# Stick-breaking attention by two sigmoids and a scan, and retention with its decay folded into q and k, in a one-core Trainium2 layer kernel

## The chip, the cores and the metric

The kernel runs on one NeuronCore of a Trainium2 chip. The metric is the device time of one launch in microseconds, median of several runs. The unchanged kernel took 957.01 us (three runs, 956.07 to 957.04).

## What is computed

One layer of a decoder with 512 tokens of 1024 features, in fp32: an RMSNorm, one wide projection, two token mixers of 8 heads each (stick-breaking attention with 64-wide heads, retention with 64-wide keys and 128-wide values), their gated merge, a convolutional GLU of width 2816, and a gated embedding. What the change touches are the two mixers:

```
# stick-breaking, strictly causal (s < t); q, k normed per head
z     = (q . k) / 8
A[t,s] = sigmoid(z[t,s]) * prod_{s<j<t} (1 - sigmoid(z[t,j]))
y     = A v
# retention, gamma_h = 1 - 2^(-5-h), q and k rotated
Y[n]  = sum_{m<=n} gamma_h^(n-m) (q_n . k_m) / 8  v_m
y_r   = rmsnorm_per_head(Y) * silu(g_r)
```

Tolerance asks for more than one fp32r pass: each operand is split into a rounded part `hi` and a rest `lo`, and each product is three matmuls (`split3`: hi.hi, hi.lo, lo.hi).

## The kernel before

Features lie on partitions, tokens along the free axis. The work is 128-column weight chunks: each chunk is eight k-steps of three matmuls of 512 columns into one of three `dense` banks. For each chunk ScalarE makes `w_hi`, VectorE `w_lo` (`ahead(j, s)` makes those of chunk s+2), SyncE loads `w_f` when the `w_lo` of two chunks earlier is done (`load`).

Heads are handled in four pairs j, with nine chunks (slots 0 to 8) a pair: stick-breaking q, k, v, retention q, k, two swish gates, two retention v. TensorE's order is written out by hand: small attention steps are hooks behind a given k-step of a given slot, written (slot, k) here. `back(j)` is slots 3 to 8 and carries the stick-breaking of pair j; `front(j)` is slots 0 to 2 and carries the retention of pair j-1. After the fourth pair, three gate chunks with the same hooks follow ("tail"). Pairs 1 to 3 are one loop, pair 0 is written apart. VectorE, ScalarE and SyncE have orders of their own, and each engine executes strictly in order, with semaphores between them.

Stick-breaking before (`sb_step`, lines 344 to 360): for one head and one block of 128 keys (8 units a pair, of 128 to 512 queries) TensorE makes z transposed (keys on partitions), and adds a mask with an extra matmul (L348). VectorE and ScalarE make softplus(z) (`sb_abs`, exp, ln, `sb_softplus`, a hi and a lo part). TensorE then adds minus the running sum over keys by matmuls with a triangular and an all-ones matrix (L358, 20 a head), ScalarE takes exp, and the weights, already transposed, go with v into `ybank` (`sb_values`). Three z banks keep three units in flight.

Retention before (`r_step`): for one head and one block of keys TensorE makes the scores, VectorE multiplies by a decay table (512 KB loaded a pair), hi and lo are made, and TensorE multiplies with v.

Rotation (`rotate`, `rotate_sum`) needs the two 32-row halves of each head exchanged. SyncE does that with four SBUF-to-SBUF DMAs (`swap_halves`, L208), which stand in its queue behind the weight load that waits for the `w_lo` of chunk 6 of the pair, which is VectorE's `ahead(j, 4)`.

Of the kernel before, what the change touches and what calls it, by code (L numbers as in the profile page):

```python
# [23 lines left out]
P = 128  # L24
# [31 lines left out]
T_SP, T_A = 27, 30  # L56
T_YQ = (28, 27)
# [8 lines left out]
A_RAW, A_SQ, A_SQY, A_SWAP, A_Y = 0, 2, (7, 3), 4, 5  # L66
A_DEC, A_COS, A_G, A_T, A_A = 8, 10, 12, 14, 16
A_SG = (10, 14, 8)
A_RS, A_ACC, A_CONV, A_C, A_SQR, A_U = 8, 9, 10, 12, 13, 16
A_RS2 = 6  # L70
A_P = 14
N_F32 = 18
H_ORDER = (0, 1, 2, 6, 4, 3, 5, 7)
# [9 lines left out]
def build(nc, xT, pT, w_in, w_a, w_b, w_out, w_up, w_down, w_pg, w_pp, g_mix, g_ffn, g_ple, g_ret, g_sbq, g_sbk,  # L83
          conv_w, conv_b, consts, decay, rope, outT):
    with ExitStack() as ctx:
# [3 lines left out]
        def sem(name):  # L89
# [10 lines left out]
        cr = sb("cr", [P, N_CONST, P], F32R)  # L100
# [23 lines left out]
        s_swap, s_rmul, s_rot, s_rhi = sem("s_swap"), sem("s_rmul"), sem("s_rot"), sem("s_rhi")  # L124
        s_misc = sem("s_misc")

        s_z, s_abs, s_e, s_l, s_sp, s_sphi, s_splo = (sem("s_z"), sem("s_abs"), sem("s_e"), sem("s_l"), sem("s_sp"),
                                                      sem("s_sphi"), sem("s_splo"))
        s_u, s_zx, s_ysum, s_yshi, s_yslo = sem("s_u"), sem("s_zx"), sem("s_ysum"), sem("s_yshi"), sem("s_yslo")
        s_ahi, s_alo = sem("s_ahi"), sem("s_alo")  # L130

        s_zr, s_zd, s_yr = sem("s_zr"), sem("s_zd"), sem("s_yr")
# [28 lines left out]
        def sb_unit(n):  # L161

            return n // NT, NT - 1 - n % NT

        def r_unit(n):

            return n // NT, n % NT

        def sp_cols(hd, i):

            at = 1280 if (hd == 1 and i == 3) else (0, 512, 896, 1152)[i]
            return at, at + width(i)

        def sp_view(t, hd, i):
            a, b = sp_cols(hd, i)
            return t[:, T_SP:T_SP + 3, :].rearrange("p t n -> p (t n)")[:, a:b]
# [5 lines left out]
        def _(sp):  # L182
# [14 lines left out]
            sp.dma_start(fs[:, A_COS:A_COS + 2, :], rope[:, :, :]).then_inc(s_rope, 16)  # L197
            for c in range(3, 8):
                load(c, c % RING, w_in[c], 8)
# [11 lines left out]
            def pair_loads(j, s):  # L211
                c = SLOTS * j + s + 5
                load(c, (s + 5) % RING, w_in[c], 8)
                if s == 4:
                    sp.wait_ge(s_h, 5)
                    swap_halves(j, 0)
                if s == 5:
                    swap_halves(j, 1)
                if s == 6:
                    sp.wait_ge(s_evac, SLOTS * j + 6)  # L220
                    sp.dma_start(fs[:, A_DEC:A_DEC + 2, :], decay[j]).then_inc(s_dec, 16)

# [62 lines left out]
        def _(pe):  # L285
# [21 lines left out]
            def stat(w, src, done):  # L307
                return mm(misc[:, :], cst[:, w, :], fs[:, src, :], start=True, stop=True).then_inc(done, 1)  # L308
# [7 lines left out]
            def stat_y(j, hd, free):  # L316

                pe.wait_ge(s_yqlo, 2 * j + hd + 1)
                pe.wait_ge(*free)
                mm(misc[:, :], cr[:, C_ONES, :], hi[:, T_YQ[hd], :], start=True, stop=False)  # L320
                mm(misc[:, :], cr[:, C_ONES, :], lo[:, T_YQ[hd], :], start=False, stop=True).then_inc(s_ystat, 1)

            def turn_v(j, s, free):
# [3 lines left out]
                for i in range(NT):  # L327
                    ins = nc.tensor.transpose(misc[:, i * P:(i + 1) * P],  # L328
                                              fs[:, A_RAW + RAW_OF[s] % 2, i * P:(i + 1) * P],
                                              cst[:, C_IDENT, :])  # L330
                ins.then_inc(s_vt, 1)

            def sb_step(j, n):

                if n < 8:
                    hd, i = sb_unit(n)
                    N = width(i)
                    if n == 0:
                        pe.wait_ge(s_raw_done, RAWS * j + 2)
                    if n >= 3:  # L340
                        pe.wait_ge(s_zx, 8 * j + n - 2)
                    rows = slice(64 * hd, 64 * hd + 64)
                    z = zbank[n % 3][:, 0:N]
                    keys, qs = slice(i * P, (i + 1) * P), slice(i * P, SEQ)
                    split3(z, hi[rows, T_SBK, keys], lo[rows, T_SBK, keys], hi[rows, T_SBQ, qs], lo[rows, T_SBQ, qs],
                           start=True, stop=False, skip=True)

                    mm(zbank[n % 3][:, 0:P], cr[:, C_IDENT, :], cr[:, C_MASK, :], start=False, stop=True,  # L348
                       skip_group_check=True).then_inc(s_z, 1)
                if n >= 2:  # L350
                    u = n - 2
                    hd, i = sb_unit(u)
                    N = width(i)
                    pe.wait_ge(s_splo, 8 * j + u + 1)
                    for ii in range(i, NT):
                        w = cr[:, C_NEGU if ii == i else C_NEG1, :]
                        for part in (hi, lo):
                            ins = mm(zbank[u % 3][:, (ii - i) * P:N], w, sp_view(part, hd, ii), start=False,  # L358
                                     stop=(ii == NT - 1 and part is lo), skip_group_check=True)
                    ins.then_inc(s_u, 1)  # L360

            def sb_values(j, v):

                _, i = sb_unit(v)
                if v == 0:
                    pe.wait_ge(s_raw_done, RAWS * j + 3)
                if v == 4:
                    pe.wait_ge(s_yslo, 2 * j + 1)
                pe.wait_ge(s_alo, 16 * j + v + 1)
                cols = slice(i * P, (i + 1) * P)  # L370
                ins = split3(ybank[:, i * P:SEQ], hi[:, T_SBV, cols], lo[:, T_SBV, cols],
                             hi[:, T_A + v % 2, 0:width(i)], lo[:, T_A + v % 2, 0:width(i)],
                             start=(v % NT == 0), stop=(v % NT == 3), skip=True)
                if v % NT == 3:
                    ins.then_inc(s_ysum, 1)

            def r_step(j, n):

                if n < 8:
                    hd, i = r_unit(n)  # L380
                    if n == 0:
                        pe.wait_ge(s_raw_done, RAWS * j + 5)
                    if n >= 3:
                        pe.wait_ge(s_zd, 8 * j + n - 2)
                    rows = slice(64 * hd, 64 * hd + 64)
                    keys, qs = slice(i * P, (i + 1) * P), slice(i * P, SEQ)
                    split3(zbank[n % 3][:, 0:width(i)], hi[rows, T_RK, keys], lo[rows, T_RK, keys], hi[rows, T_RQ, qs],
                           lo[rows, T_RQ, qs], start=True, stop=True).then_inc(s_zr, 1)
                if n >= 1:
                    v = n - 1  # L390
                    hd, i = r_unit(v)
                    if v == 0:
                        pe.wait_ge(s_yslo, 2 * j + 2)
                        pe.wait_ge(s_raw_done, RAWS * j + 6)
                    if v == 4:
                        pe.wait_ge(s_raw_done, RAWS * j + 7)
                        pe.wait_ge(s_yraw, 2 * j + 1)
                    pe.wait_ge(s_alo, 16 * j + 8 + v + 1)
                    cols = slice(i * P, (i + 1) * P)
                    ins = split3(ybank[:, i * P:SEQ], hi[:, T_RV + hd, cols], lo[:, T_RV + hd, cols],  # L400
                                 hi[:, T_A + v % 2, 0:width(i)], lo[:, T_A + v % 2, 0:width(i)],
                                 start=(i == 0), stop=(i == 3), skip=True)
                    if i == 3:
                        ins.then_inc(s_yr, 1)
# [4 lines left out]
            def front(j, prev):  # L409

                for s in range(3):
                    free_bank(j, s)
                    hooks = {1: lambda: r_step(prev, 3 * s), 4: lambda: r_step(prev, 3 * s + 1),
                             7: lambda: r_step(prev, 3 * s + 2)}
                    if s == 0:
                        hooks[6] = lambda: turn_v(prev, 8, (s_raw_done, RAWS * j - 1))
                    if s == 1:
                        hooks[5] = lambda: stat_qk(j, 0, (s_raw_done, RAWS * j))
                    if s == 2:
                        hooks[3] = lambda: stat_qk(j, 1, (s_misc, 4 * j - 1))  # L420
# [1167 lines left out]
```

## Time and profile before

| | us |
|---|---|
| median of three runs | 957.01 |
| span of the profiled execution | 955.7 |
| TensorE matmul busy | 941.7 |
| VectorE busy | 522.8 |
| ScalarE busy | 433.9 |

The span runs from the first to the last instruction of the profiled execution. The 1.3 us between it and the median lie around it. Matmuls are pipelined and overlap in the trace, so the duration of one says less than the distance from its start to the start of the next.

### The profile page before, as it was taken

How to read it: one execution, taken by the hardware profiler on the slowest of the kernel's cores; microseconds unless marked ns; L12 is line 12 of the kernel's file. 1: busy time of each engine (PE TensorE's matmuls, PEld its weight loads, DVE VectorE, ACT ScalarE, POOL GpSimd, SP SyncE). 2: the span in 40 equal slices, each digit the busy share in tenths (PEclk: the TensorE clock that was granted, in tenths of full speed). 3: DMA queues.
4: the chain of work that ended last, by engine and by line, in shares of the span. 5: the costliest groups of instructions: out<-in, count | busy, mean ns of one | idle time of the engine just before them, and what ended most of it. 6: DMA issues, size and time to landing. Idle time of an engine off the chain costs nothing.

```text
span 955.7 us, 12085 instructions
## 1 busy us (share of the span) xinstructions
PE 941.7 (99%) x4214; PEld 756.9 (79%) x4214; DVE 522.8 (55%) x741; ACT 433.9 (45%) x662; POOL 4.0 (0%) x11
## 2 busy tenths in 40 slices
PE   6999999999999999999999999999999999999998
PEld 4777778778777878888878788888888888888786
DVE  6887575566566544333355565655656553333354
ACT  6566676477566644222334533333333332222422
POOL 1000000000000000000000000000000000000000
PEclk9999999999999999999999999999999999999999
DMA  7232122122213114332232233232232333332232
GB/s 258 70 110 67 57 77 88 44 77 89 75 44 110 50 50 177 117 103 78 86 124 97 90 109 110 88 107 90 88 108 89 98 89 99 88 96 87 76 122 82
DMA packets 27851, 89.95 MB, mean 94 GB/s; under 512 B 3728, under 2 KB 4768, under 8 KB 27696
## 3 DMA queue, kind: packets, MB, share of 16 engines
q1 hardware_dynamic: 27168, 86.91, 27.9%
q10 hardware_dynamic: 432, 2.63, 0.8%
q8 instruction: 16, 0.26, 0.1%
q0 software_dynamic: 224, 0.06, 0.0%
q14 instruction: 11, 0.09, 0.0%
HBM read 85.39 MB, written 2.10 MB: 92 GB/s over the span
## 4 chain that ended last, share of the span: by engine, by line
PE 96%; DVE 2%; ACT 1%; DMA 1%; issue 0%; SPq 0%; DVEq 0%; ACTq 0%
PE dense L290 28%; PE dense L292 27%; PE dense L291 27%; PE z L290 2%; PE z L358 2%; PE ybank L290 2%; PE z L292 1%; PE ybank L291 1%; PE z L291 1%; PE ybank L292 1%; PE z L348 1%; PE misc L308 1%; DVE fs L1009 1%; DMA fs<-in_xT 1%; PE misc L328 1%; DVE w_lo L1009 1%
## 5 line engine op out<-in xcount | busy, mean ns | idle before, releaser
L290 PE MATMUL dense<-hi,w_hi 128*128 128x512 f32 x1184 | 472.0, 399 | 9.8 <-DVE lo L1012 9.4
L291 PE MATMUL dense<-lo,w_hi 128*128 128x512 f32 x1184 | 462.6, 391 | 0.0
L292 PE MATMUL dense<-hi,w_lo 128*128 128x512 f32 x1184 | 462.4, 391 | 0.0
L1009 DVE TENSOR_TENSOR w_lo<-w_f,w_hi 128x1024 fp32r<-128x1024 f32 (+2 forms) x160 | 184.5, 1153 | 241.8 <-ACT w_hi L581 241.5
L290 PEld LDWEIGHTS dense<-hi,w_hi 128*128 128x128 f32 x1184 | 223.2, 189 | 57.7 <-issue 12.8
L292 PEld LDWEIGHTS dense<-hi,w_lo 128*128 128x128 f32 x1184 | 222.9, 188 | 47.2
L291 PEld LDWEIGHTS dense<-lo,w_hi 128*128 128x128 f32 x1184 | 223.3, 189 | 45.3 <-issue 2.6
L581 ACT CAST w_hi<-w_f 128x1024 fp32r<-128x1024 f32 (+2 forms) x160 | 158.3, 990 | 184.2 <-PE dense L292 182.1
L566 ACT ACTIVATE fs<-fs 128x512 f32<-128x512 f32 (+5 forms) x151 | 87.1, 580 | 99.6 <-DVE fs L1009 41.8
L1009 DVE TENSOR_TENSOR lo<-fs,hi 128x512 fp32r<-128x512 f32 (+4 forms) x167 | 94.5, 576 | 56.7 <-ACT hi L944 20.1
L1009 DVE TENSOR_TENSOR fs<-fs 128x512 f32<-128x512 f32 x99 | 67.4, 687 | 2.5 <-DMA fs<-fs 0.3
L1009 DVE TENSOR_TENSOR fs<-dense,fs 128x512 f32<-128x512 f32 x84 | 57.5, 684 | 8.7 <-ACT fs L566 5.0
L1012 DVE SCALAR_TENSOR_TENSOR fs<-fs,cw 128x512 f32<-128x512 f32 x44 | 33.1, 752 | 28.0 <-ACT fs L566 25.0
L944 ACT CAST hi<-fs 128x512 f32 (+1 forms) x22 | 13.7, 621 | 59.5 <-DVE fs L1009 59.5
L566 ACT ACTIVATE fs<-fs,cw 128x512 f32<-128x512 f32 x22 | 17.9, 816 | 43.8 <-DVE fs L1009 43.8
L1009 DVE TENSOR_TENSOR fs<-z,fs 128x512 f32<-128x512 f32 (+3 forms) x32 | 15.7, 489 | 31.2 <-PE z L292 31.2
L647 ACT CAST hi<-fs 128x512 fp32r<-128x512 f32 (+3 forms) x32 | 14.7, 460 | 38.4 <-DVE fs L1009 38.4
L1012 DVE SCALAR_TENSOR_TENSOR lo<-fs,gain,hi 128x512 fp32r<-128x512 f32 (+1 forms) x24 | 17.7, 750 | 25.1 <-ACT hi L566 25.1
L290 PEld LDWEIGHTS z<-hi 64*128 64x128 f32 x64 | 11.7, 183 | 23.0 <-issue 22.1
L290 PE MATMUL z<-hi 64*128 64x128 f32 (+3 forms) x64 | 26.2, 410 | 0.2 <-DVE lo L1009 0.2
L1012 DVE SCALAR_TENSOR_TENSOR fs<-z,fs 128x128 f32<-128x128 f32 (+3 forms) x32 | 15.7, 489 | 16.0 <-ACT fs L566 15.8
L290 PE MATMUL ybank<-hi 128*128 128x128 f32 (+3 forms) x64 | 22.6, 353 | 0.0
(67 smaller groups left out, 497.9 us busy)
## 6 DMA issues: line engine op xcount, KB each, us to landing
w_f<-in_w_in SPq DMA_DIRECT2D x52, 512.0 KB, 3.3
w_f<-in_w_up SPq DMA_DIRECT2D x44, 512.0 KB, 3.2
w_f<-in_w_down SPq DMA_DIRECT2D x16, 512.0 KB, 3.5
w_f<-in_w_b SPq DMA_DIRECT2D x8, 512.0 KB, 3.3
w_f<-in_w_out SPq DMA_DIRECT2D x8, 512.0 KB, 3.3
w_f<-in_w_pg SPq DMA_DIRECT2D x8, 512.0 KB, 3.3
w_f<-in_w_down SPq DMA_DIRECT2D x8, 384.0 KB, 3.0
fs<-in_xT SPq DMA_DIRECT2D x4, 512.0 KB, 7.6
```

The lines of the kernel that those rows point to most:

```text
L290: mm(out, w1, x1, start=start, stop=False, skip_group_check=skip)
L291: mm(out, w1, x0, start=False, stop=False, skip_group_check=skip)
L292: return mm(out, w0, x1, start=False, stop=stop, skip_group_check=skip)
L308: return mm(misc[:, :], cst[:, w, :], fs[:, src, :], start=True, stop=True).then_inc(done, 1)
L328: ins = nc.tensor.transpose(misc[:, i * P:(i + 1) * P], fs[:, A_RAW + RAW_OF[s] % 2, i * P:(i + 1) * P], cst[:, C_IDENT, :])
L358: ins = mm(zbank[u % 3][:, (ii - i) * P:N], w, sp_view(part, hd, ii), start=False, stop=(ii == NT - 1 and part is lo), skip_group_check=True)
L566: return nc.scalar.activation(out, src, func, **kw).then_inc(done, 1)
L581: nc.scalar.copy(w_hi[r][:, 0:kt, :], w_f[r][:, 0:kt, :]).then_inc(s_whi, 1)
L647: nc.scalar.copy(hi[:, T_A + n % 2, 0:width(i)], fs[:, A_A + n % 2, 0:width(i)]).then_inc(s_ahi, 1)
L944: nc.scalar.copy(hi[:, T_G + f, :], fs[:, A_U, :]).then_inc(s_ghi, 1)
L1009: return nc.vector.tensor_tensor(out, a, b, op).then_inc(done, 1)
L1012: return nc.vector.scalar_tensor_tensor(out=out, in0=a, scalar=scalar, in1=b, op0=op0, op1=op1).then_inc(done, 1)
```

## The change

Stick-breaking now works on a block of 128 queries (i = 3, 2, 1, 0), with queries on partitions and all its keys (512, 384, 256, 128) along the free axis, for both heads of the pair at once. The scores of the two heads alternate matmul by matmul, one on array rows 0 to 63, the other on 64 to 127, into two banks `z`. ScalarE takes sigmoid(z) into SBUF and sigmoid(-z) in place in PSUM. VectorE scans the latter over the keys from the last to the first (one `tensor_tensor_scan` a head, 511 to 127 elements) and multiplies. TensorE transposes the weights back with the identity (20 transposes of 128 x 128 a pair), ScalarE and VectorE make hi and lo, and the value matmuls are those of before. The mask matmul, the triangular sums, and the softplus go.

Retention: q is multiplied by gamma^t and k by its inverse (`decayed`), so that the scores need only a 128 x 128 causal mask on the diagonal block. Both heads go together here too. The decay table shrinks to two rows of factors (`load_fac`). The steps behind retention (`y_raw`, `y_square`, `norm_y`, `y_swish`, `low_y`) take both heads in one instruction. A preload of the sigmoid tables is added a pair. There is one z buffer where there were three.

The core of the diff:

```diff
+            def heads_scores(i, w, x, cols, at):
+                for (wp, xp), first, last in (((hi, hi), True, False), ((hi, lo), False, False),
+                                              ((lo, hi), False, True)):
+                    for hd in range(2):
+                        rows = slice(64 * hd, 64 * hd + 64)
+                        ins = mm(z[:, hd, 0:cols.stop - cols.start], wp[rows, w, i * P:(i + 1) * P], xp[rows, x, cols],
+                                 start=first, stop=last)
+                ins.then_inc(at, 1)
...
+            def sb_scores(j, i):
...
+                    pe.wait_ge(s_scan, 8 * j + 2 * (NT - 1 - i))
...
+            def sb_turn(j, i):
...
+                    pe.wait_ge(s_atlo, NT * j + (NT - 1 - i))
+                pe.wait_ge(s_a, NT * j + NT - i)
...
+                places = {(5, 2): at(sb_scores, j, 2), (5, 4): at(sb_turn, j, 3), (5, 7): at(sb_scores, j, 1),
+                          (6, 1): at(sb_turn, j, 2), (6, 2): at(sb_values, j, 0, 3), (6, 3): at(sb_scores, j, 0),
+                          (6, 5): at(sb_turn, j, 1), (6, 6): at(sb_values, j, 0, 2), (7, 0): at(sb_turn, j, 0),
+                          (7, 2): at(sb_values, j, 0, 1), (7, 4): at(sb_values, j, 0, 0), (7, 7): at(sb_values, j, 1, 3),
+                          (8, 0): at(sb_values, j, 1, 2), (8, 1): at(sb_values, j, 1, 1), (8, 2): at(sb_values, j, 1, 0),
+                          (8, 6): at(turn_v, j, 7, (s_atlo, NT * j + NT))}
...
+                    places[3, 3] = at(turn_v, j, 2, (s_misc, 3 * j + 1))
+                    places[3, 4] = at(sb_scores, j, 3)
+                    places[3, 7] = at(stat_y, prev, (s_raw_done, RAWS * j + 3))
...
+            def sb_factors(j, i):
+
+                n = NT - 1 - i
+                act.wait_ge(s_z, NT * j + n + 1)
+                if n or not isinstance(j, int):
+                    act.wait_ge(s_tr, NT * j + n)
+                zz = z[:, :, 0:keys(i)]
+                run(fs[:, A_AT:A_AT + 2, 0:keys(i)], zz, ACT.Sigmoid, s_beta)
+                act.wait_ge(s_beta, NT * j + n + 1)
+                run(zz, zz, ACT.Sigmoid, s_f, scale=-1.0)
...
             def back(j, prev):
                 evac(j, 2)
                 ahead(j, 3)
-                sb_early(j, 0)
                 high_v(j, 0)
...
+                norm_y(prev, 3 * j + 2)
+                sigmoid_tables()
+                evac(j, 3)
+                sb_factors(j, 3)
+                high_y(prev)
                 ahead(j, 4)
...
                 evac(j, 4)
+                sb_factors(j, 2)
+                sb_high(j, 3)
                 ahead(j, 5)
...
+            def sb_weights(j, i):
...
+                for hd in range(2):
+                    nc.vector.tensor_tensor_scan(fs[:, A_CP + hd, 1:N], z[:, hd, N - 1:0:-1], mrev[:, 0:N - 1], 0.0,
+                                                 ALU.mult, ALU.max).then_inc(s_scan, 1)
+                dve.wait_ge(s_scan, 8 * j + 2 * n + 2)
+                a = fs[:, A_AT:A_AT + 2, 0:N]
+                tt(a, a, fs[:, A_CP:A_CP + 2, N - 1::-1], ALU.mult, s_a)
...
+            def turned(j, t):
+                rotate(j, t)
+                rotate_sum(j, t)
+                decayed(j, t)
...
             def back(j, prev):
                 ahead(j, 3)
...
                 low_v(j, 0)
+                y_norm(prev)
+                y_swish(prev)
+                sb_weights(j, 3)
+                low_y(prev)
+                ahead(j, 4)
+                turned(j, 0)
+                sb_weights(j, 2)
+                sb_low(j, 3)
+                ahead(j, 5)
+                low_rot(j, 0)
+                sb_weights(j, 1)
+                sb_low(j, 2)
+                sb_weights(j, 0)
+                ahead(j, 6)
+                sb_low(j, 1)
+                turned(j, 1)
                 sb_low(j, 0)
...
```

## Rows read from the trace of the kernel before

**Rows 1.** The page: engine totals, granted clock by slices, chain that ended last.

```profile
PE 941.7 (99%) x4214; PEld 756.9 (79%) x4214; DVE 522.8 (55%) x741; ACT 433.9 (45%) x662; POOL 4.0 (0%) x11
...
PEclk9999999999999999999999999999999999999999
...
PE 96%; DVE 2%; ACT 1%; DMA 1%; issue 0%; SPq 0%; DVEq 0%; ACTq 0%
```

**Rows 2.** TensorE's waits: waiter, whom it waited for, total us, times, longest.

```profile
PE dense L290 <- DVE lo L1012: 9.4, 3, 8.7
```

**Rows 3.** TensorE timeline (start, us, instruction): last matmuls before borders of phases.

```profile
81.94 0.40 PE L292 MATMUL ybank<-hi,lo 128*128 128x512 f32 x1
...
111.83 0.27 PE L292 MATMUL ybank<-hi,lo 128*128 128x128 f32 x1
...
193.10 0.27 PE L292 MATMUL ybank<-hi,lo 128*128 128x128 f32 x1
...
353.94 0.27 PE L292 MATMUL ybank<-hi,lo 128*128 128x128 f32 x1
```

**Rows 4.** TensorE timeline around a score step, a transpose group, mask and triangular sums.

```profile
83.31 0.39 PE L292 MATMUL dense<-hi,w_lo 128*128 128x512 f32 x1
...
84.85 0.40 PE L291 MATMUL dense<-lo,w_hi 128*128 128x512 f32 x1
...
116.20 0.60 PE L328 MATMUL misc<-cst,fs 128*128 128x128 f32 x4
116.55 0.48 PE L290 MATMUL dense<-hi,w_hi 128*128 128x512 f32 x1
116.87 0.39 PE L291 MATMUL dense<-lo,w_hi 128*128 128x512 f32 x1
...
136.83 0.33 PE L348 MATMUL z<-cr 128*128 128x128 f32 x1
137.00 0.45 PE L358 MATMUL z<-hi,cr 128*128 128x512 f32 x1
...
137.52 0.34 PE L358 MATMUL z<-hi,cr 128*128 128x384 f32 x1
...
137.87 0.28 PE L358 MATMUL z<-hi,cr 128*128 128x256 f32 x1
...
138.11 0.23 PE L358 MATMUL z<-hi,cr 128*128 128x128 f32 x1
...
138.28 0.45 PE L290 MATMUL dense<-hi,w_hi 128*128 128x512 f32 x1
```

**Rows 5.** Instruction groups by shape, first 360 us: busy us, mean ns | idle.

```profile
L566 ACT ACTIVATE fs<-fs 128x512 f32<-128x512 f32 x49 | 30.5, 629 | 5.2 <-DVE fs L1152 4.2
L566 ACT ACTIVATE fs<-fs 128x1024 f32<-128x1024 f32 x4 | 4.2, 1059 | 0.0
L570 ACT ACT_TABLE_LOAD x5 | 6.4, 1283 | 1.3 <-DVE eps L1020 1.2
...
L1009 DVE TENSOR_TENSOR w_lo<-w_f,w_hi 128x1024 fp32r<-128x1024 f32 x41 | 50.2, 1224 | 24.1 <-ACT w_hi L581 23.9
L1009 DVE TENSOR_TENSOR lo<-fs,hi 128x512 fp32r<-128x512 f32 x57 | 38.9, 688 | 23.6 <-ACT hi L689 12.5 <-ACT hi L647 6.4 <-ACT hi L630 2.1
```

**Rows 6.** Timelines of VectorE and SyncE, pair 0: w_lo, exchange DMAs, first use.

```profile
46.65 1.23 DVE L1009 TENSOR_TENSOR w_lo<-w_f,w_hi 128x1024 fp32r<-128x1024 f32 x1 [0.26 <-ACT w_hi L581]
...
48.51 2.50 SPq L208 DMA_DIRECT2D fs<-fs  x4
...
52.67 1.29 DVE L1009 TENSOR_TENSOR fs<-fs 128x512 f32<-128x512 f32 x2 [0.29 <-DMA fs<-fs]
```

**Rows 7.** TensorE timeline at the start: the first matmul, and where spacing changes.

```profile
8.68 0.77 PE L290 MATMUL dense<-hi,w_hi 128*128 128x512 f32 x1 [8.68 <-DVE lo L1012]
...
14.79 0.40 PE L292 MATMUL dense<-hi,w_lo 128*128 128x512 f32 x1
15.03 0.40 PE L290 MATMUL dense<-hi,w_hi 128*128 128x512 f32 x1
```

More of the change, by code:

```diff
@@ L55 @@
 T_RQ, T_RK, T_RV = 23, 24, 25
-T_SP, T_A = 27, 30
-T_YQ = (28, 27)
+T_AT = 27
+T_YQ = 27
 T_X0 = 8
@@ L159, in a_sq, with keys, flat, at_blocks @@
             return A_T + t if isinstance(j, int) else A_SQ
[L161 to L176, printed above, removed]
+        def keys(i):
+            return P * (i + 1)
+        def flat(t):
+            return t[:, T_AT:T_AT + 5, :].rearrange("p t n -> p (t n)")
+        def at_blocks(t):
+            return flat(t).rearrange("p (h b c) -> p h b c", h=2, b=10)
+        def at_row(t, hd, kb):
+            first = 10 * hd + (0, 4, 8, 7)[kb]
+            return flat(t)[:, first * P:first * P + width(kb)]
+        def r_pair(t, i):
+            at = T_AT + 2 * (i % 2)
+            return t[:, at:at + 2, 0:width(i)]
+        def yq(t):
+            return t[:, T_YQ:T_YQ + 2, :]
+        def norm_y_pair():
+            return fs[:, A_SQY:A_SQY + 5:4, :]
         block = ctx.enter_context(nc.Block())
@@ L331, in turn_v @@
                 ins.then_inc(s_vt, 1)
[L333 to L360, printed above, removed]
@@ L374, in sb_values @@
[L374 to L404, printed above, removed]
@@ new lines, in sb_values, with r_scores @@
+                pe.wait_ge(s_atlo, NT * j + NT - kb)
+                cols = slice(kb * P, (kb + 1) * P)
+                ins = split3(aty[:, 2, kb * P:SEQ], hi[:, T_SBV, cols], lo[:, T_SBV, cols], at_row(hi, hd, kb),
+                             at_row(lo, hd, kb), start=(kb == NT - 1), stop=(kb == 0), skip=True)
+                if kb == 0:
+                    ins.then_inc(s_ysum, 1)
+            def r_scores(j, i):
+                if i == 0:
+                    pe.wait_ge(s_raw_done, RAWS * j + 5)
+                    pe.wait_ge(s_scan, 8 * j + 8)
+                else:
+                    pe.wait_ge(s_ralo, NT * j + i)
+                heads_scores(i, T_RK, T_RQ, slice(i * P, SEQ), s_zr)
@@ new lines, in r_values @@
+            def r_values(j, i):
+                if i == 0:
+                    pe.wait_ge(s_yslo, 2 * j + 2)
+                    pe.wait_ge(s_atlo, NT * j + NT)
+                    pe.wait_ge(s_raw_done, RAWS * j + 7)
+                pe.wait_ge(s_ralo, NT * j + i + 1)
+                cols = slice(i * P, (i + 1) * P)
+                for hd in range(2):
+                    ins = split3(aty[:, 1 + hd, i * P:SEQ], hi[:, T_RV + hd, cols], lo[:, T_RV + hd, cols],
+                                 r_pair(hi, i)[:, hd, :], r_pair(lo, i)[:, hd, :], start=(i == 0), stop=(i == NT - 1),
+                                 skip=True)
+                ins.then_inc(s_vr, 1)
@@ L411, in front @@
                 for s in range(3):
                     free_bank(j, s)
[L413 to L420, printed above, removed]
-                        hooks[6] = lambda: stat_y(prev, 0, (s_misc, 4 * j))
@@ L422, in front @@
[L422 to L436 removed]
+                    chunk(first_chunk + s, s, s, KD, T_H, {k: places[s, k] for k in range(KD) if (s, k) in places})
@@ L462, in _ @@
             with pe.Fori(1, PAIRS) as j:
-                front(j, j - 1)
+                front(j, j - 1, SLOTS * j)
                 back(j, j - 1)
             last = PAIRS - 1
-            for s in range(3):
-                free_bank(PAIRS, s)
-                hooks = {1: lambda: r_step(last, 3 * s), 4: lambda: r_step(last, 3 * s + 1),
-                         7: lambda: r_step(last, 3 * s + 2)}
-                if s == 0:
-                    hooks[5] = lambda: turn_v(last, 8, (s_raw_done, RAWS * PAIRS - 1))
-                if s == 2:
-                    hooks[3] = lambda: stat_y(last, 0, (s_raw_done, RAWS * PAIRS))
-                chunk(GATE0 + s, s, s, KD, T_H, hooks)
+            front(PAIRS, last, GATE0, tail=True)
             pe.wait_ge(s_gate, 1)
-            chunk(GATE0 + 3, 0, 0, KD, T_H, {3: lambda: stat_y(last, 1, (s_misc, 4 * PAIRS - 1))})
+            chunk(GATE0 + 3, 0, 0, KD, T_H, {5: lambda: stat_y(last, (s_raw_done, RAWS * PAIRS))})
             def branch_a(c, r, m):
@@ L738, in front @@
-                y_square(prev, 0)
-                evac(j, 1)
-                r_high(prev, 6)
                 high_qk(j, 0)
-                norm_qk(j, 1, 4 * j)
-                r_high(prev, 7)
+                ahead(j, 2)
+                norm_qk(j, 1, 3 * j + 1)
+                y_raw(prev)
                 high_qk(j, 1)
-                ahead(j, 2)
-                norm_y(prev, 0, 4 * j + 1)
-                y_raw(prev, 1)
-                y_square(prev, 1)
+                y_square(prev)
@@ new lines, in y_norm, with y_swish @@
+            def y_norm(j):
+                dve.wait_ge(s_yrs, j + 1)
+                for hd in range(2):
+                    y = fs[:, A_Y + hd, :]
+                    col = G_RET + hd + 2 * j
+                    stt(y, y, gain[:, col, :], norm_y_pair()[:, hd, :], ALU.mult, ALU.mult, s_yn)
+            def y_swish(j):
+                y = fs[:, A_Y:A_Y + 2, :]
+                dve.wait_ge(s_silu, j + 1)
+                dve.wait_ge(s_yn, 2 * j + 2)
+                tt(y, y, fs[:, A_G:A_G + 2, :], ALU.mult, s_yf)
@@ new lines, in low_y @@
+            def low_y(j):
+                dve.wait_ge(s_yrhi, j + 1)
+                pair = bass.ds(T_YR + 2 * j, 2)
+                tt(lo[:, pair, :], fs[:, A_Y:A_Y + 2, :], hi[:, pair, :], ALU.subtract, s_yrlo)
+            def sb_weights(j, i):
+                n = NT - 1 - i
+                N = keys(i)
+                dve.wait_ge(s_f, NT * j + n + 1)
+                if n or not isinstance(j, int):
+                    dve.wait_ge(s_a, NT * j + n)
+                for hd in range(2):
+                    nc.vector.tensor_tensor_scan(fs[:, A_CP + hd, 1:N], z[:, hd, N - 1:0:-1], mrev[:, 0:N - 1], 0.0,
[3 more added lines that the diff above has]
+                tt(a, a, fs[:, A_CP:A_CP + 2, N - 1::-1], ALU.mult, s_a)
@@ L1303, in back @@
-                ahead(j, 5)
-                sb_step(j, 5)
-                low_rot(j, 0)
-                ahead(j, 6)
-                sb_step(j, 6, lambda: y_low(j, 0))
-                sb_step(j, 7, lambda: rotate(j, 1), lambda: rotate_sum(j, 1))
+                y_norm(prev)
[7 more added lines that the diff above has]
+                ahead(j, 5)
```

560 lines of the change are left out of this document (243 added, 317 removed).

## The prediction

> **What bounds the kernel now.** First the page: TensorE is busy 99% of the span and makes 96% of the chain that ended last [rows 1]. Busy time of pipelined matmuls can hide waits, so next the list of TensorE's waits: one large one, 8.7 us before the first matmul, and almost nothing after it [rows 2]. The hand-written order covers every wait, so time is the sum of matmul spacings, and a microsecond taken from TensorE's work would be one gained if the cover held. Third, the phase borders [rows 3]. Slot 3 of pair 1 starts behind 111.83, that of pair 2 behind 193.10: a pair takes 81.3 us. Slot 0 of pair 1 starts at 82.2 (81.94 and one spacing), so a front takes 29.8 and a back 51.5. The attention is over at 354, behind 353.94; what follows isn't changed. A dense matmul of 512 columns is spaced 0.227 us, a k-step is 0.68, a slot 5.46.
>
> **What TensorE loses and gains** [rows 4]. Mask: 136.83 to 137.00, 0.17 each, 8 a pair: 1.4. Triangular sums, a hi and a lo matmul each: 0.52 for 512 columns (137.00 to 137.52), 0.35 for 384, 0.24 for 256, 0.17 for 128. A head needs 1, 2, 3 and 4 of these: 2.62; two heads 5.2. Score step: from 83.31 to 84.85 lie 1.54 us with two dense spacings in them, so a 512-column step costs 1.09: three matmuls of 0.227, and 0.41 for going to 64-row matmuls and back. With 0.17, 0.12 and 0.11 for the shorter ones, four steps of a head cost 3.5 and a mixer's two heads 7.0.
>
> After the change a mixer has four entries instead of eight. No row shows two matmuls on different array halves. If head 1 costs nothing beside head 0, a mixer costs 3.5; if they queue up, 3.5 + 1.9 = 5.4. I take 3.5: operands lie on separate row halves, results in separate banks, and nothing in a 64-row matmul uses the other half. The Trainium skill (TensorE: Matmul & The Clock Gate, Part 3) has such matmuls start nearly together; no run here shows it yet.
>
> Added transposes: 116.20 to 116.55 is 0.0875 each, the next dense one comes 0.09 late; 20 in four groups: 2.1. Values, statistics and v transposes keep their matmuls. Saved a pair: 1.4 + 5.2 + 2 x 3.5 - 2.1 = 11.5, of it 3.5 in the front; four pairs 46 us. A pair would be 69.8.
>
> **Whether the cover holds.** ScalarE costs about 0.20 + 0.84 ns an element, a table load 1.28, VectorE 0.15 + 1.05 ns an element [rows 5]. In total both get less: stick-breaking takes two sigmoids and a cast where it took five passes, and one scan, one product and one subtraction where it took four. But the work is now one chain with one z buffer: the scores of block i wait for both scans of block i+1, the sigmoids wait for that block's transposes. Three units in flight hid this before.
>
> The scan has no row. Below is one tensor_tensor: 0.69 for 512. Above I take two cycles an element, since each result needs a multiply and then a max of the one before it: 0.15 + 2 x 1.05 ns, so 1.23, 0.96, 0.69, 0.42 us for 512 to 128. I use the upper end. The Trainium skill (DVE: opcode table, instruction layouts, handler registers and perf-mode slots, Datapath and trigger behaviour) says the built-in scan runs at half throughput. Its figure would be this same 1.23; no row bears on it.
>
> A steady back, zero at the end of slot 3, where `stat_y` has just run. ScalarE, strictly in order: `norm_y` (two of 1024) to 2.4, sigmoid tables 3.7, `evac` 4.2, two sigmoids of 1024 to 6.4. VectorE: two scans to 8.8, product 10.0, `low_y` 11.2, `ahead(j, 4)` 12.4. That last one releases the SyncE load with the four exchange DMAs behind it, and VectorE's next instruction, `rotate`, wants them landed. From the end of that `w_lo` (46.65 + 1.23 = 47.9) to the first rotation, which waited for the DMA at 52.67, are 4.8 us [rows 6]. Before, this lay under other work; now VectorE stands to 17.2. Rotation and decay (four of 0.69) last to 20.2, and only then come the scans of block 2, to 22.1. Behind the waiting instruction are queued these scans, `sb_low(j, 3)` and `ahead(j, 5)`.
>
> TensorE meanwhile: slot 4 to 5.5, three k-steps to 7.5, waits 1.3 for the first scans, scores 0.9, two k-steps, transposes 0.8, three k-steps: 13.9. Its scores of block 1 at (5, 7) wait for the scans at 22.1: **8.2 us**. Further on: at (6, 3) two sigmoids of 512 and two scans of 256 take 2.85 behind the transposes, covered by 1.7: 1.15. At (7, 0) 3.9 (sigmoids, scans, product, `ahead`, `sb_low(j, 1)`) are covered by 2.4: 1.5. At (7, 7) the values of head 1 wait for `y_low`, behind a silu with table loads on both sides: 1.6. At (3, 3) `turn_v` waits for an `evac` behind `y_square`: 0.4. Sum 14.2 a pair, against 11.5 saved.
>
> Pair 0 has another order, with scans of block 2 ahead of the rotation. There I walk to 1.8 at (5, 7), 5.2 at (6, 3) (the rotation, `ahead` and `evac_x` stand before its scans), 0.5 at (7, 0) and 3.5 at (7, 7): 11. The tail keeps its cover: `stat_y` to `low_y` is some 7.3 us, against 8.2 us of matmuls.
>
> **The clock.** After its 8.7 us of standing idle TensorE ran 14 spacings in 6.1 us, 0.43 each, which is 512 columns at 1.2 GHz, and then 0.24 and 0.23, at 2.4 GHz [rows 7]. The page's granted clock doesn't show it, its first slice is as full as all others [rows 1]. That start lost 14 x 0.2 = 2.9 us. A wait of 8.2 us resembles it; some of the loss is taken up by the waits just behind, so I count 2.0 a pair and 1.0 in pair 0: 7 us. The bounds are 0 and 4 x 2.9 = 12. The Trainium skill (TensorE: Matmul & The Clock Gate, Part 1) says that an idle array goes back to half clock. That rule speaks against this change: without it the sum below ends 7 us lower.
>
> **The sum** against the profiled 955.7: -46 + 3 x 14.2 + 11 + 7 = +14.6, a span of 970.3. The median lies 1.3 above the span: 971.6, say 971.5. The smaller decay load (DMA queues are mostly idle) and the added constants at the start, where VectorE has 8 us of matmuls ahead of it, I put at nothing; without that cover the latter would be 2 us.
>
> **The rivals.**
> - *The long wait is short; faster.* One mechanism: VectorE comes to the scans of block 2 earlier. If the scan streams like a tensor_tensor, each pair's waits fall by 2.6 (10 us in all), and then, with the exchange landed within 3.2 us instead of 4.8, by 1.6 more in three pairs (5); TensorE stands less than 6 us at a time and the clock stays up (7). 971.5 - 22 = 949.5. It decides where a pair's waits sum to less than 11.5, that is, where the wait at (5, 7) is under 5.5 us. For it: every wait here is from a walk of four queues, and back-to-back instructions overlap by 0.1. Against it: the exchange is tied to `ahead(j, 4)` and VectorE stands right behind it. Chance 0.22.
> - *The two heads queue up.* 1.9 a mixer more, in the fronts on TensorE, in the backs on the chain: 15 more, 986.5. For it: no row shows overlap. Chance 0.13.
> - *TensorE's work alone counts*, as it does before: 957 - 46 = 911. Against it is the single z buffer. Chance 0.04.
> - *Losses meet gains*, within 0.2%: 957. Chance 0.05.
> - The forecast, 971.5 with its own range from 960 (fast scan) to 980: chance 0.56.
>
> **How the numbers follow.** Faster is 0.22 + 0.04 = 0.26, same 0.05, slower 0.56 + 0.13 = 0.69. About 0.2% is what a measurement of this kernel can tell from no change. The range runs from 946, which takes in the faster rival and leaves out the lone TensorE case, to 988, which takes in the queueing heads.
>
> **What would show it.** Right: TensorE's largest waits are z <- DVE scan, about 8 us three times, with VectorE idle for 4 to 5 us on DMA fs<-fs just before; a pair of about 86 us; scans of 1.2 us for 512; matmuls spaced 0.43 behind the long waits; the two heads' score matmuls starting nearly together. Wrong: a wait at (5, 7) under 5.5 us, scans of 0.7, or spacing of 0.227 straight after the wait. A pair below 81 us makes the sign wrong.

## The result, and the profile after

The changed kernel takes 971.3 us (median of 4 runs, 968.87 to 973.42) against 956.96 (4 runs) for the kernel before on the same chip. The ratio is 1.0152, with a 95% interval of 1.0135 to 1.017: slower by 14.4 us, where 971.5 was forecast. The profiled execution spans 969.4 us against 955.7. This is its page (engine totals, granted clock by slices, chain that ended last); it answers to [rows 1]:

```profile
PE 908.7 (94%) x4102; PEld 733.5 (76%) x4102; DVE 511.8 (53%) x653; ACT 395.8 (41%) x517; POOL 4.0 (0%) x11
...
PEclk9999989998999999999999999999999999999999
...
PE 81%; ACT 7%; DVE 6%; issue 3%; DMA 1%; SPq 1%; ACTq 0%; DVEq 0%
```

TensorE, VectorE and ScalarE all have less to do than before, and yet the span grew. TensorE went from 99% busy to 94%, and its share of the chain from 96% to 81%; what it lost went to ScalarE, VectorE, the issue of instructions and the exchange DMA. Two slices of the clock row show an 8. All of it lies in the first 370 us, the attention.

TensorE's waits (waiter, whom it waited for, total us, times, longest). Before there was one group that mattered [rows 2]:

```profile
PE z L366 <- DVE fs L1155: 33.9, 11, 7.4
...
PE dense L314 <- DVE lo L998: 9.0, 3, 8.3
PE aty L314 <- DVE lo L995: 7.6, 4, 3.1
PE aty L393 <- DVE lo L995: 5.2, 4, 1.5
```

`PE dense L314` is the old wait ahead of the first matmul. The other three are new, 46.7 us together: scores waiting for the scan, values and transposes waiting for a low half.

The phase borders of [rows 3] are now here (TensorE timeline: start, us, instruction):

```profile
112.21 0.27 PE L316 MATMUL aty<-hi,lo 128*128 128x128 f32 x1
...
197.39 0.27 PE L316 MATMUL aty<-hi,lo 128*128 128x128 f32 x1
```

A pair takes 85.2 us (197.39 - 112.21, and 85.3 for the next one, which ends at 282.69) instead of 81.3: 3.9 more. The last matmul of the attention starts at 366.05 where it did at 353.94, 12.1 later. The border isn't at the same place in the order, though: from it to the first matmul of the same later stage (496.16 before, 509.85 after), the windows hold 626 and 634 matmuls. Columns: window, us, PE busy (count), PEld, DVE, ACT, POOL, clock, DMA share, GB/s; first before, then after.

```profile
353.94:496.16 142.22, 141.82 (x626) 116.83 (x626) 57.81 (x69) 47.92 (x62) 0.00 (x0) 1.00 0.34 113
```

```profile
366.05:509.85 143.80, 143.40 (x634) 118.41 (x633) 58.49 (x67) 49.97 (x61) 0.00 (x0) 1.00 0.32 112
```

Both are full but for 0.4 us, and the second is 1.6 longer, by eight more matmuls: the same work, cut at another place. So 12.1 + 1.6 = 13.7 is what the attention costs more, and it is all of the difference of the spans. Three pairs of 3.9 and 2.0 in pair 0 make it up.

Now one back, that of pair 1, on TensorE. The last bracket is the idle time before the row, and who ended it:

```profile
130.73 0.44 PE L366 MATMUL z<-hi 64*128 64x384 f32 x2 [1.06 <-DVE fs L1155]
...
143.34 0.58 PE L366 MATMUL z<-hi 64*128 64x256 f32 x2 [7.27 <-DVE fs L1155]
...
144.28 0.79 PE L314 MATMUL dense<-hi,w_hi 128*128 128x512 f32 x1
144.87 0.63 PE L315 MATMUL dense<-lo,w_hi 128*128 128x512 f32 x1
145.29 0.63 PE L316 MATMUL dense<-hi,w_lo 128*128 128x512 f32 x1
...
147.84 0.39 PE L315 MATMUL dense<-lo,w_hi 128*128 128x512 f32 x1
148.06 0.39 PE L316 MATMUL dense<-hi,w_lo 128*128 128x512 f32 x1
...
150.43 0.33 PE L366 MATMUL z<-hi 64*128 64x128 f32 x2 [0.94 <-DVE fs L1155]
...
156.96 0.43 PE L393 MATMUL aty<-cst,fs 128*128 128x128 f32 x2 [1.52 <-DVE lo L995]
...
164.97 0.33 PE L314 MATMUL aty<-hi 128*128 128x128 f32 x1 [1.52 <-DVE lo L995]
```

Five waits, 12.3 us. Behind the long one the dense matmuls start 0.42 apart (144.87, 145.29; the next two 0.43 each) and by 147.84 are 0.22 apart again. Here the granted clock shows it, which it didn't at the start [rows 7] (windows, columns as above; 0.52 here, 1.00 again from 147 to 150):

```profile
143.30:147.00 3.70, 3.66 (x13) 2.81 (x14) 3.68 (x5) 0.00 (x0) 0.00 (x0) 0.52 0.01 2
```

And VectorE with SyncE's queue over the same stretch; it answers to [rows 6]:

```profile
128.34 2.33 DVE L1155 TENSOR_TENSOR_SCAN fs<-z,mrev 128x511 f32<-128x511 f32 x2 [1.06 <-ACT z L586]
...
131.85 1.22 DVE L995 TENSOR_TENSOR lo<-fs,hi 128x1024 f32 x1
132.99 1.22 DVE L995 TENSOR_TENSOR w_lo<-w_f,w_hi 128x1024 fp32r<-128x1024 f32 x1
138.83 2.02 DVE L995 TENSOR_TENSOR fs<-fs 128x512 f32<-128x512 f32 x3 [4.62 <-DMA fs<-fs]
...
141.49 1.79 DVE L1155 TENSOR_TENSOR_SCAN fs<-z,mrev 128x383 f32<-128x383 f32 x2
```

```profile
134.38 0.33 SPq L203 DMA_DIRECT2D w_f<-in_w_in  x1
134.84 2.46 SPq L232 DMA_DIRECT2D fs<-fs  x4
```

VectorE ends its `w_lo` at 134.2. Only then does SyncE issue the weight load and, behind it, the four exchange DMAs. VectorE's next instruction wants them and stands 4.6 us; rotation and decay follow, then the scans of block 2 to 143.3, and at 143.34 TensorE gets its scores. Two scans of 511 take 2.33.

### The profile page after: what moved, and what is told of

Its sections match the earlier page's. It is cut to its first block, busy times and chain, and to the rows that moved or that the text cites. A ratio compares the mean times of both kernels' runs of the same rounds, so it can differ in the third digit from the quotient of the medians.

```text
span 969.4 us, 11519 instructions
## 1 busy us (share of the span) xinstructions
PE 908.7 (94%) x4102; PEld 733.5 (76%) x4102; DVE 511.8 (53%) x653; ACT 395.8 (41%) x517; POOL 4.0 (0%) x11
## 4 chain that ended last, share of the span: by engine, by line
PE 81%; ACT 7%; DVE 6%; issue 3%; DMA 1%; SPq 1%; ACTq 0%; DVEq 0%
PE dense L314 25%; PE dense L316 24%; PE dense L315 24%; ACT fs L586 2%; PE z L366 2%; DVE fs L1155 2%; DVE fs L995 1%; DVE w_lo L995 1%; DVE lo L995 1%; ACT w_hi L601 1%; PE aty L314 1%; PE aty L332 1%; PE aty L316 1%; PE aty L315 1%; ACT z L586 1%
## 5 line engine op out<-in xcount | busy, mean ns | idle before, releaser
L314 PE MATMUL dense<-hi,w_hi 128*128 128x512 f32 x1184 | 476.6, 402 | 9.4 <-DVE lo L998 9.0
L314 PEld LDWEIGHTS dense<-hi,w_hi 128*128 128x128 f32 x1184 | 224.2, 189 | 62.7 <-issue 16.5
L995 DVE TENSOR_TENSOR fs<-fs 128x512 f32<-128x512 f32 (+3 forms) x115 | 82.9, 726 | 18.9 <-DMA fs<-fs 13.7
L586 ACT ACTIVATE fs<-fs 128x512 f32<-128x512 f32 (+2 forms) x79 | 55.4, 707 | 81.1 <-DVE fs L995 42.0
L995 DVE TENSOR_TENSOR lo<-fs,hi 128x512 fp32r<-128x512 f32 (+3 forms) x63 | 48.1, 765 | 41.5 <-ACT hi L930 20.1
L366 PE MATMUL z<-hi 64*128 64x512 f32 (+3 forms) x64 | 13.9, 432 | 34.0 <-DVE fs L1155 33.9
L366 PEld LDWEIGHTS z<-hi 64*128 64x128 f32 x64 | 6.3, 194 | 46.4 <-DVE fs L1155 38.6
L930 ACT CAST hi<-fs 128x512 f32 (+1 forms) x22 | 13.7, 621 | 59.5 <-DVE fs L995 59.5
L1155 DVE TENSOR_TENSOR_SCAN fs<-z,mrev 128x511 f32<-128x511 f32 (+3 forms) x32 | 24.5, 807 | 18.9 <-ACT z L586 18.8
L998 DVE SCALAR_TENSOR_TENSOR fs<-fs,gain 128x512 f32<-128x512 f32 x24 | 17.5, 748 | 29.6 <-ACT fs L586 29.6
L586 ACT ACTIVATE fs<-z 128x1024 f32<-128x1024 f32 (+3 forms) x16 | 11.3, 706 | 45.8 <-PE aty L393 45.8
L670 ACT CAST hi<-z 128x1024 fp32r<-128x1024 f32 (+3 forms) x16 | 11.1, 694 | 40.9 <-DVE z L995 40.9
```

Source lines behind the costliest of these rows:

```text
L314: mm(out, w1, x1, start=start, stop=False, skip_group_check=skip)
L366: ins = mm(z[:, hd, 0:cols.stop - cols.start], wp[rows, w, i * P:(i + 1) * P], xp[rows, x, cols], start=first, stop=last)
L586: return nc.scalar.activation(out, src, func, **kw).then_inc(done, 1)
L670: nc.scalar.copy(r_pair(hi, i), z[:, :, 0:width(i)]).then_inc(s_rahi, 1)
L930: nc.scalar.copy(hi[:, T_G + f, :], fs[:, A_U, :]).then_inc(s_ghi, 1)
L995: return nc.vector.tensor_tensor(out, a, b, op).then_inc(done, 1)
```

## Experiments

The theory: the loss is one chain in each back (exchange, rotation, scans, scores), whose cost is a wait of some 7 us and the clock behind it; TensorE's work really is smaller, and the two heads overlap. The rivals: the heads don't overlap; they do so only as neighbours in the program; the rotation itself, not the exchange, is what is late; the clock costs nothing; the waits belong to the new form and can't be covered.

### The exchange ahead of the weight load

```
             c = SLOTS * j + s + 5          # on SyncE
-            load(c, (s + 5) % RING, w_in[c], 8)
             if s == 4:
                 sp.wait_ge(s_h, 4)
                 swap_halves(j, 0)
+            load(c, (s + 5) % RING, w_in[c], 8)
             if s == 5:
                 swap_halves(j, 1)
```

Only in slot 4 does the order change: the exchange of `q` goes ahead of the load, that of `k` in slot 5 stays behind it. The exchange reads the retention `q` as ScalarE copied it out of the `dense` bank, and that is there well before the ring's buffer is free.

> Edit: SyncE issues the four exchange DMAs of pair j's q ahead of the weight load that waits for chunk 6's w_lo, no longer behind it. Theory (VectorE stands for the exchange in front of the scans of block 2): VectorE's 4.6 us of waiting for DMA fs<-fs vanish, TensorE's wait at (5, 7) falls from 7.3 to about 2.6 us in pairs 1 to 3, matmuls behind it stay at 0.227 apart, so 4.7 + 1 us a pair: about 955 instead of 971. Rival (one z buffer and one weight buffer make the chain of scores, sigmoids, scans and transposes too long by itself; the exchange only fills time that would be waited anyway): the wait at (5, 7) stays above 5.5 us, time 967 or more.

956.2 us, ratio 0.9997 (0.9987 to 1.0007): level with the kernel before, 15.1 less than the changed one. SyncE now issues the exchange at 127.31, where it was 134.84, and the first rotation follows its predecessor at once (SyncE, then VectorE):

```profile
127.31 2.46 SPq L232 DMA_DIRECT2D fs<-fs  x4
```

```profile
133.93 1.22 DVE L995 TENSOR_TENSOR w_lo<-w_f,w_hi 128x1024 fp32r<-128x1024 f32 x1
135.07 2.02 DVE L995 TENSOR_TENSOR fs<-fs 128x512 f32<-128x512 f32 x3
```

The long wait fell from 7.3 to 2.6 in all three pairs (the third is 2.59 at 298.76). Of the others only two are shorter, the 0.95 behind it in pair 2 (0.40) and the 0.65 in pair 0 (not in the list any more). TensorE timeline:

```profile
139.58 0.39 PE L366 MATMUL z<-hi 64*128 64x256 f32 x2 [2.56 <-DVE fs L1155]
...
218.78 0.39 PE L366 MATMUL z<-hi 64*128 64x256 f32 x2 [2.59 <-DVE fs L1155]
```

Three times 4.7 is 14 of the 15 us. So the order of two entries in SyncE's queue decides between slower and level. Not all of the clock came back, which the windows behind the three waits show (columns as above): in pair 1 it stays up, in pairs 2 and 3 it doesn't. From border to border the three pairs are 5.9, 5.3 and 4.7 us shorter (79.3, 80.0 and 78.7), so beyond the waits it was pair 1 that got something back, 1.2, and the others at most 0.2. Pair 0 ended 0.9 later, as more matmuls behind its waits ran slowly.

```profile
139.50:146.00 6.50, 5.44 (x34) 4.01 (x35) 5.82 (x10) 2.00 (x4) 0.00 (x0) 1.00 0.28 88
218.70:226.00 7.30, 6.82 (x34) 5.33 (x35) 5.83 (x10) 2.01 (x4) 0.00 (x0) 0.77 0.31 104
298.70:306.00 7.30, 6.30 (x31) 4.82 (x31) 5.37 (x9) 1.99 (x4) 0.00 (x0) 0.77 0.34 100
```

### The rotation behind the next unit

```
-                turned(j, 0)
                 ...            # scans of block 2 and sb_low(j, 3)
+                turned(j, 0)
```

> Edit: VectorE's rotation and decay of q in pairs 1 to 3 move behind the scans and the lo parts of block 2, as in pair 0; nothing else. Theory: the wait at (5, 7) falls to about 1.5 to 2 us, but ScalarE's rounding of the rotated q stands ahead of block 1's sigmoids, so the wait at (6, 3) grows from 0.9 to about 4.3; sum 3.5 less a pair and no slow matmuls, 957 to 960. Rival (chain too long by itself): the wait at (5, 7) stays above 5.5, 968 or more.

961.9 us, ratio 1.0063 (1.0047 to 1.008), a little above the 957 to 960 expected. VectorE does the scans while the exchange is under way. The long wait is 1.6, and one of 3.5 stands at the next scores:

```profile
136.19 0.39 PE L366 MATMUL z<-hi 64*128 64x256 f32 x2 [1.57 <-DVE fs L1155]
...
144.59 0.33 PE L366 MATMUL z<-hi 64*128 64x128 f32 x2 [3.53 <-DVE fs L1155]
```

The expectation had no slow matmuls either; behind the 3.53 the granted clock was 0.69 (144.5 to 150). The reason for the wait is on ScalarE, which works strictly in order: its `high_rot`, the cast of the rotated block, stands ahead of the next sigmoids, and now waits for the later rotation.

```profile
141.02 0.62 ACT L654 CAST hi<-fs 128x512 fp32r<-128x512 f32 x1 [4.78 <-DVE fs L995]
...
142.02 0.60 ACT L586 ACTIVATE fs<-z 128x512 f32<-128x512 f32 x1
```

Two cures of the same wait, by different means, bring 15 and 9 us. Both leave the rotation's four instructions as long as they were, and the first also leaves them where they were, ahead of the scans: so it is the exchange that was late. What one engine gains by a step moved back, the engine that takes its result next has to pay for, if its own order stays.

### Filling the wait

Ahead of the wait at (5, 7) TensorE gets 28 matmuls whose results nobody reads, in pairs 1 to 3. They change nothing that is waited for.

```
+                    if i == 1 and not isinstance(j, int):
+                        pe.wait_ge(s_yraw, j)
+                        for _ in range(28):
+                            mm(aty[:, 2, :], ones_r[:, :], hi[:, T_H, :], start=True, stop=True)
```

> Edit: in pairs 1 to 3, 28 matmuls of 512 columns with no use (6.4 us at 0.227) are put in front of the wait at (5, 7), into a bank that is overwritten afterwards; the output is unchanged. Theory (idling drops the clock): the scores behind the wait and the six dense matmuls after them stay at 0.227 instead of 0.43, about 1.5 us a pair less: 966 to 968. Rival (the slow spacing is no matter of idling, or the lost time is covered by the next wait): 971, within 1.5.

966.8 us, ratio 1.0115 (1.0098 to 1.0132): 4.6 less than the changed kernel, by adding work. In the profiled spans it is 964.0 against 969.4, 5.4 less. What is left of the wait is 0.98, and the dense matmuls behind it start 0.23 apart behind the first one (TensorE timeline):

```profile
142.15 0.39 PE L366 MATMUL z<-hi 64*128 64x256 f32 x2 [0.98 <-DVE fs L1159]
...
143.04 0.39 PE L315 MATMUL dense<-lo,w_hi 128*128 128x512 f32 x1
143.27 0.39 PE L316 MATMUL dense<-hi,w_lo 128*128 128x512 f32 x1
```

From border to border the three pairs take 84.0, 83.9 and 81.9 us instead of 85.2, 85.3 and 83.4, which puts the price of the clock alone at 1.2 to 1.5 us a pair. The other 1.2 of the 5.4 lie in pair 0, where the program is the same in both kernels: there behind the wait of 3.06 the clock stayed up in this execution and fell in the other. The experiment also confirms that the end of the wait is set elsewhere, since TensorE could do 28 more matmuls in it.

### The heads in turn, and the heads apart

First, all three matmuls of head 0 and then those of head 1 (before: the two heads alternate):

```
-                for (wp, xp), first, last in ...:
-                    for hd in range(2):
+                for hd in range(2):
+                    for (wp, xp), first, last in ...:
```

> Edit: the six score matmuls of a block run head 0's three first, then head 1's three, where they alternated. Theory (heads overlap only if neighbours in the order lie on different array halves): a mixer costs 1.9 us more on TensorE, 7.5 in the four fronts and a like amount on the chain in the backs: 979 to 986. Rival (TensorE overlaps what it finds in its queue, in whatever order, or the overlap is worth nothing): 971, within 2.

971.8 us, ratio 1.0161 (1.0144 to 1.0178), as the changed kernel. The rows are a surprise: in this program head 1's first matmul stands behind all of head 0's, and still the two first ones form one group, ahead of the second ones.

```profile
87.20 0.39 PE L316 MATMUL dense<-hi,w_lo 128*128 128x512 f32 x1
87.52 0.51 PE L366 MATMUL z<-hi 64*128 64x512 f32 x2
87.85 0.41 PE L366 MATMUL z<-lo,hi 64*128 64x512 f32 x2
88.08 0.41 PE L366 MATMUL z<-hi,lo 64*128 64x512 f32 x2
88.42 0.51 PE L314 MATMUL dense<-hi,w_hi 128*128 128x512 f32 x1
88.76 0.40 PE L315 MATMUL dense<-lo,w_hi 128*128 128x512 f32 x1
```

From the dense matmul ahead to the second one behind are 1.56 us (88.76 - 87.20), 1.55 in the changed kernel, and 1.54 with one head in the kernel before [rows 4]. So the heads ran side by side in either order, and the theory's half sentence that they have to be neighbours fell. The edit thus couldn't price the overlap, and a second one had to keep them apart: head 1 comes one dense k-step after head 0.

```
+                one_head(0)
+                late.append(lambda: one_head(1).then_inc(at, 1))   # run behind the next k-step
```

> Edit: in every block of scores, stick-breaking's and retention's, head 1's three matmuls come one dense k-step after head 0's, so that a full-array matmul stands between the halves; all else as in the changed kernel. Theory (the halves share time, in whatever order they stand, as long as nothing of the full array lies between them; a mixer of 3.5 us becomes the 7.0 of the kernel before): 14 us more in the four fronts, and in the backs 0.7 to 1.7 us more in front of each of four links of the chain, 12 to 18 us over four pairs: 995 to 1005. Rival (the overlap is worth little, the entries were the price): 975 to 983.

999.3 us, ratio 1.0456 (1.0439 to 1.0474), within the 995 to 1005 expected. Each head is now a step of its own:

```profile
91.80 0.49 PE L370 MATMUL z<-hi 64*128 64x512 f32 x1
...
93.59 0.50 PE L370 MATMUL z<-hi 64*128 64x512 f32 x1
```

The span grew by 27.5 us although the waits of the scores shrank by 6.0 (27.9 instead of 33.9). That is 33.5 us for 32 more steps, 1.05 each, where the forecast's 3.5 for four steps of all sizes gives 0.88. Of the rest, some 5 us, half is the clock: behind the long waits 7 or 8 dense spacings are slow where 5 were, 2.0 to 2.2 us above 0.227 in sum and not 1.2, which is 2.6 in three pairs and leaves about 1.0 a step. The other half isn't traced. Side by side, the second head costs nothing that can be seen.

### All orders

Is 11.5 us a pair of TensorE's work saved, and are the waits a matter of order alone? The last kernel computes the same with the same instructions, in another order: the exchange ahead of the load as above, and each unit of the back given more cover.

```
 back, TensorE:  scores of block 1 (5, 7) -> (6, 1), of block 0 (6, 3) -> (6, 7)
                 transposes (6, 1) -> (6, 3), (6, 5) -> (7, 2), (7, 0) -> (7, 5)
                 values of head 1 (7, 7)..(8, 2) -> (8, 4)..(8, 7); stat_y (3, 7) -> (3, 5)
 VectorE:        turned(j, 0) behind sb_low(j, 1), turned(j, 1) behind y_low(j, 0),
                 ahead(j, 6) ahead of sb_weights(j, 0), low_v ahead of ahead(j, 3)
 ScalarE:        high_rot(j, 0) behind sb_high(j, 0), y_high(j, 0) and the evac ahead of silu,
                 high_rot(j, 1) behind silu, high_v ahead of ahead(j, 3)
```

This is the edit in short; the values of head 0 move to match, and pair 0 has the same pattern.

> Edit: orders alone. The exchange DMAs ahead of the weight load; VectorE's rotations and ScalarE's rounding of rotated q and k behind the chain of scans; `stat_y` at (3, 5); the hooks of blocks 2 to 0 spread over slots 5 to 8, so that every link of the chain has 2 to 4 k-steps of cover; silu and its table loads behind the rounding of head 0's output. Theory (TensorE's saved work is real and only the waits ate it): a pair of 70 to 73 us instead of 85, waits under 3 us a pair, 918 to 932 us, faster than both kernels. Rival (the chain is too long for its six slots whatever the order): waits of 6 us or more a pair remain, 945 or more.

918.7 us, ratio 0.9609 (0.9593 to 0.9625): 37.5 us faster than the kernel before on the same chip (956.2), 52.6 faster than the changed one, by order alone. TensorE's waits are

```profile
PE dense L314 <- DVE lo L1002: 9.1, 3, 8.4
PE aty L393 <- DVE lo L999: 1.5, 4, 0.4
...
PE z L366 <- DVE fs L1159: 1.0, 5, 0.2
```

and a whole pair, at full clock throughout:

```profile
124.35:196.04 71.69, 70.92 (x353) 55.04 (x354) 46.97 (x62) 42.67 (x60) 0.00 (x0) 1.00 0.25 77
```

A pair is 71.7, with 0.6 of waits in it, so TensorE's work in a pair is 71.1 and the saving 81.3 - 71.1 = 10.2.

## Why the prediction was right

The number came out within 0.2 us. Its terms did not, though the mechanism did: one chain of exchange, rotation, scans and scores, whose waits eat more than TensorE saves. This is how they stand (us, in the profiled execution, with the sign of what they add):

```
                                       forecast   measured
TensorE's work, 4 pairs                 -46.0      -40.8   (-10.2 each)
waits, pairs 1 to 3                     +42.6      +36.8   (12.3 each)
waits, pair 0                           +11.0       +9.9
clock                                    +7.0       +7.8   (the rest; 1.8 each and 2.3)
span                                    +14.6      +13.7
```

The rest of pair 0 also holds the start, where the wait ahead of the first matmul was 0.4 shorter (8.29 and not 8.68).

*The saving: 11.5 forecast, 10.2 measured.* This step was mis-sized. Going to 64-row matmuls and back was priced at 0.41 for all 16 head steps of a pair, but in 8 of them the matmul behind the step was the mask. Its 0.17 [rows 4] was priced whole, and held part of the way back: among the values 128 columns take 0.06 to 0.11. So 0.05 to 0.1 for each of the 8 was counted twice. The transposes cost 1.95 and, at the next matmuls, 0.4, instead of 2.1. Summing the spacings of a pair by kind, before and in the last kernel, gives the split: the triangular sums and the mask were worth 6.7, the overlap of heads 5.8 and not 7.0.

*The overlap.* It was taken from no row. The groups of two starting together and the kernel with the heads apart show it: 27.5 us of span hang on it.

*The long wait: 8.2 forecast; 7.27, 7.36 and 7.03 measured.* The mechanism was right in each link: VectorE idle for 4.62 against 4.8 on the exchange, behind `w_lo`, with the weight load ahead of it in SyncE's queue; the first experiment takes it away and 15 us with it.

*The scan: 1.23 forecast, 1.21 measured* for 511 elements, 0.94 for 383 (means of eight each). Twice the 1.05 ns an element of a tensor_tensor was the right end of the bounds; this is the line that shows it (instruction groups by shape, first 380 us; busy, mean ns of one | idle before, and its releaser):

```profile
L1155 DVE TENSOR_TENSOR_SCAN fs<-z,mrev 128x511 f32<-128x511 f32 x8 | 9.3, 1209 | 3.3 <-ACT z L586 3.2
```

*The smaller waits: 1.3, 1.15, 1.5, 1.6 forecast; 1.06, 0.94, 1.52, 1.52 measured.* The walk was good to 0.3 each, and its errors were nearly all on the long side. A likely reason, argued only: back-to-back instructions start up to 0.1 before the end of the one before (131.85 + 1.22 is 133.07, and the next one started at 132.99), and there are a dozen of them ahead of the long wait. For 1.15 it is a slip: two sigmoids of 512 and two scans of 256 come to 2.64 at the prediction's own prices, not 2.85, and 2.64 less the cover of 1.7 is the 0.94 that was measured. The wait of 0.4 at (3, 3) doesn't appear in the list of waits.

*Pair 0: 1.8, 5.2, 0.5, 3.5 forecast; 1.56, 4.67, 0.65, 3.06 measured.* The different order there moves the long wait to (6, 3), as said. The clock took 1.0 in the sum. It took more: it fell twice, behind the 4.67 and behind the 3.06, which the first two windows show. The third is the same stretch of the kernel with the filled wait, whose program is the same in pair 0: it waited 3.06 at that place too, and its clock stayed up.

```profile
61.40:66.00 4.60, 4.53 (x19) 3.65 (x20) 2.23 (x4) 0.00 (x0) 0.00 (x0) 0.63 0.44 147
78.20:82.10 3.90, 3.87 (x13) 3.29 (x14) 2.31 (x3) 0.07 (x1) 0.00 (x0) 0.56 0.45 173
```

```profile
78.50:82.00 3.50, 3.42 (x19) 3.03 (x20) 2.36 (x4) 0.12 (x1) 0.00 (x0) 1.00 0.42 150
```

*The clock in the other pairs: 2.0 forecast.* Filling the wait gives 1.2 to 1.5 a pair. What is left over in the table is 1.8, so 0.3 to 0.6 of that isn't shown to be the clock.

*Errors that met.* The saving was 5.2 too large, the waits 6.9 too large, the clock 0.8 too small, which leaves the span 0.9 below the forecast (969.4 and not 970.3). The prediction then added 1.3 for what lies around the span, and in the profiled execution it was 1.8 (971.2 and 969.4). The hit within 0.2 us is partly luck, and an error of 5 was in the range. The sign wasn't luck: it hung on waits of more than 10.2 a pair, and they were 12.3.

*The rivals.* "The long wait is short" was a single edit away: it is what the first experiment made, and it came to 956, not 949.5, since the scan doesn't stream like a tensor_tensor and the clock still fell in two pairs. It had taken the clock to stay up where TensorE stands less than 6 us; it fell behind 4.67, 3.06 and 2.59. "The heads queue up" is ruled out. "TensorE's work alone counts", 911, was given 0.04; the last experiment shows its price to have been low by the 5.2 of the saving, and that such a kernel exists at 918.7. Its objection, the single `z` buffer, doesn't hold in principle: the buffer only asks for more distance between units than the order gave.

Left open: what decides on the clock behind a wait of 2.6 to 3.1 us. It isn't the wait's length alone, for it stayed up behind 2.6 in pair 1 of the first experiment and not in pairs 2 and 3, and behind the 3.06 to 3.09 of pair 0 it fell in the changed kernel and the first experiment and stayed up in the three with the heads in turn, the later rotation and the filled wait. Open too is how much each edit of the last kernel, beyond the exchange, brings of the 37.5 us between it and the first experiment.

## What to carry to other kernels

A change that shortens every engine's work can still lose when it turns independent units into one chain: lay out the chain with all four queues before trusting the sum of work, and look at what is queued ahead of each DMA, since here two entries of SyncE's queue were worth 15 us. Cover is a matter of order, and order costs nothing: spread the units until each wait falls under the matmuls between them, on all engines together, as a step moved on one engine alone moves the wait to the next. When a price is read off between two neighbours of different kinds, ask whether the neighbour's price holds it already.

## What the runs showed of the hardware that wasn't expected

- Matmuls of 64 rows on different halves of the array ran side by side in either program order, also when two others of head 0 stood between them in the program (1.55 and 1.56 us across the step of 512); about 1.0 us for each further step when dense matmuls kept them apart.
- The clock of TensorE fell also behind waits of 4.67 us (0.63 granted in the stretch behind it), and of 2.6 in two of three cases (0.77, with one of 1.06 eight us earlier), besides those of 7 us (0.50 to 0.54). Behind the same wait of 3.1 us at the same place it read 0.56 and 0.50 in two kernels and 1.00 in three. Behind waits of 1.0 to 1.6 it read 1.00 in pair 1 of the changed kernel, but 0.76 behind one of 1.57 in pair 3 with the later rotation.
- The granted clock reads 1.00 over the first matmuls, which ran 0.43 apart [rows 7], and 0.52 over matmuls equally far apart in the middle of the kernel. The spacing is the safer witness. How many of the first matmuls run slowly differs from one execution to the next: the spacings near 0.43 between dense matmuls at the start number 14 in the kernel before, 12 in the changed one and 7 to 9 in the six experiments, which is 2.9 us of the span at most and 1.5 at least.
